# Expert gathers of 8 KB rows into one ring, in groups of two slots, in a decoder-step kernel on one core

## The reference, cut to what matters

```
q = (x @ w_query).reshape(t, 8, 2, 128);  s = einsum('thcd,ckd->thck', q, sub_keys)
sv, si = top_k(s, 16)                          # 16 best of 128 keys, twice a head
cand = sv[:, :, 0, :, None] + sv[:, :, 1, None, :];  top_s, pos = top_k(cand, 16)
experts = ...;  g = softmax(top_s)
u = expert_u[experts];  v = expert_v[experts]  # rows of 1024 float32, 4 KB each
a = gelu(einsum('td,thkd->thk', x, u))
out = einsum('thk,thkd->td', g * a, v)
```

## Time and profile before

| what | value |
|---|---|
| runs | 4222.06, 4222.38, 4271.96 us |
| span of the profiled execution | 4238.2 us |
| busy in the span | PE 81%, DVE 56%, POOL 56%, ACT 20% |
| DMA | 1320.95 MB, mean 312 GB/s |
| prompt front alone, ahead of tile 0 | 256.6 us |
| tile 7, 3564 to 4165 us | PE busy 502.5 of 601 us, DMA share 0.82 |
| one tile of the loop | 463 to 482 us (from one copy of `pick_cur` at L1316 to the next: 256.6, 737.5, 1200.6, 1675.3, 2149.4, 2618.9, 3093.0, 3564.0) |

### The profile page before, as it was taken

The page is one execution under the profiler, slowest core; times in us unless marked ns, Lnnn a source line. Parts: engine busy times, 40 slices in busy tenths (PEclk is TensorE's granted clock), DMA queues, the critical chain, the costliest instruction groups (busy, mean ns, idle before and its releaser), DMA issues.

```text
span 4238.2 us, 46989 instructions
## 1 busy us (share of the span) xinstructions
PE 3438.5 (81%) x13488; PEld 1997.5 (47%) x13488; DVE 2356.8 (56%) x5378; ACT 867.9 (20%) x2023; POOL 2390.2 (56%) x2071
## 2 busy tenths in 40 slices
PE   7749887798869886997879886998879886989874
PEld 5625453455435543654435543644445443733341
DVE  2464457455854476444854476455844466255666
ACT  1111211222121212122122212121122212122211
POOL 0036565666656575666656575665666566355642
PEclk9879998899989998998989998998889988699976
DMA  4369799989989798989989898989989898788884
GB/s 161 105 218 373 270 352 348 335 309 355 393 293 355 268 371 318 372 289 337 387 292 357 288 382 303 371 300 328 367 315 348 296 382 317 258 306 294 290 299 165
DMA packets 540672, 1320.95 MB, mean 312 GB/s; under 512 B 59252, under 2 KB 271774, under 8 KB 540376
## 3 DMA queue, kind: packets, MB, share of 16 engines
q0 software_dynamic: 297216, 1082.26, 69.2%
q1 hardware_dynamic: 239636, 229.70, 16.5%
q10 hardware_dynamic: 3524, 5.57, 0.4%
HBM read 1311.77 MB, written 5.62 MB: 311 GB/s over the span
## 4 chain that ended last, share of the span: by engine, by line
PE 42%; DVE 28%; issue 16%; another core or an unknown queue 5%; DMA 4%; ACT 4%; SPq 1%; DVEq 1%; POOL 0%; ACTq 0%; POOLq 0%
PE acc L690 18%; DVE u_ring L1280 12%; PE front L419 7%; PE front L526 3%; PE front L575 3%; DMA w_ring<-in_w_o 2%; PE front L547 2%; ACT diag L939 2%; PE front L527 2%; DVE si_u L1181 1%; DVE sv L1180 1%; PE front L650 1%; DMA w_ring<-in_w_in 1%; DVE work L1181 1%
## 5 line engine op out<-in xcount | busy, mean ns | idle before, releaser
L690 PE MATMUL acc<-v_ring,diag 128*128 128x512 f32 x3880 | 1889.3, 642 | 278.5 <-ACT diag L939 216.7
L1427 POOL DMA_INDIRECT v_ring<-in_expert_v,pick_cur x1024 | 1243.2, 1214 | 1054.9 <-PE acc L690 720.2
L1427 POOL DMA_INDIRECT u_ring<-in_expert_u,pick_cur x1024 | 1122.9, 1097 | 740.3 <-issue 306.5
L690 PEld LDWEIGHTS acc<-v_ring,diag 128*128 128x128 f32 x3880 | 781.0, 207 | 1251.2 <-issue 1137.8
L1280 DVE CUSTOM_DVE_ANT_0 u_ring<-u_ring,xn_cur 128x1024 f32<-128x1024 f32 x1024 | 1198.7, 1221 | 110.7 <-DMA u_ring<-in_expert_u,pick_cur 82.0
L419 PE MATMUL front<-work,w_ring 128*128 128x128 f32 (+1 forms) x4896 | 632.2, 285 | 74.7 <-issue 48.9
L419 PEld LDWEIGHTS front<-work,w_ring 128*128 128x128 f32 x4896 | 613.4, 204 | 103.6 <-issue 74.4
L930 ACT ACTIVATE gelu<-dots 128x4 f32<-128x4 f32 x256 | 52.6, 206 | 1508.1 <-DVE dots L1280 1401.6
L939 ACT ACTIVATE diag<-ident,wgt 128x128 f32<-128x128 f32 x970 | 310.4, 390 | 139.0 <-DVE wgt L1286 126.9
L575 PE MATMUL front<-w_ring,work 128*128 128x256 f32 (+1 forms) x576 | 158.2, 444 | 66.4 <-DVE work L1148 32.7
L1180 DVE MAX8 sv<-work 128x8 f32<-128x128 f32 (+1 forms) x288 | 83.2, 289 | 200.6 <-issue 113.9
(11 more groups left out here) (245 smaller groups left out, 2592.0 us busy)
## 6 DMA issues: line engine op xcount, KB each, us to landing
w_ring<-in_w_in SPq DMA_DIRECT2D x72, 1024.0 KB
w_ring<-in_w_query SPq DMA_DIRECT2D x72, 1024.0 KB
w_ring<-in_w_o SPq DMA_DIRECT2D x36, 1024.0 KB
u_ring<-in_expert_u,pick_cur POOLq DMA_INDIRECT x1024
v_ring<-in_expert_v,pick_cur POOLq DMA_INDIRECT x1024
work<-in_cache_ckv SPq DMA_DIRECT2D x64, 128.0 KB
w_ring<-in_w_in SPq DMA_DIRECT2D x9, 768.0 KB
x_t<-in_x_prompt SPq DMA_DIRECT2D x8, 512.0 KB
```

The costliest lines, as they stand in the source:

```text
L690: last = nc.tensor.matmul(acc[:, half, :], diag[:, slot, :], v_ring[:, slot, half * 512:half * 512 + 512], start=False, stop=(g == GROUPS ...
L1427: pool.indirect_dma_start(ring[:, slot, :], None, a[table][0], bass.IndirectOffsetOnAxis(ap=pick, axis=0)).then_inc(loaded[slot], 16)
```

## The change

Ahead of the launch, `expert_u` and `expert_v` are laid side by side in one table with rows of 8 KB. The kernel has one ring of 8 slots of 8 KB (`uv_ring`; `u_ring` and `v_ring` are its halves), one semaphore a slot and one gather a slot. That gather waits until the v product of the slot eight before is done. `G` goes from 4 to 2, so a tile has 64 groups of two slots; the order within a group stays as it was, and so does the number of slots in the ring, 8. `beside` now puts a prompt stage beside every second group (norm 0, turn 2, latent 4, ..., query 0 to 4 at 40 to 48, select 0 at 50, query 5 to 8 at 52 to 58, select 1 at 60) and, in tile 7, one stage beside each of the groups 0 to 61. The samples' mixer at the end gathers 8 rows of 8 KB a partition, all of them after the last v product of tile 7.

```diff
-G = 4
+G = 2
 GROUPS = SLOTS // G
-RING = 2 * G
+RING = 8
+ROUNDS = SLOTS // RING
...
-        u_ring = sb("u_ring", [P, RING, D])
-        v_ring = sb("v_ring", [P, RING, D])
+        uv_ring = sb("uv_ring", [P, RING, 2 * D])
...
+        u_ring, v_ring = uv_ring[:, :, 0:D], uv_ring[:, :, D:2 * D]
...
             def v_group(it, g):
                 for r in range(G):
-                    slot = (g % 2) * G + r
-                    if by_vector(it, g * G + r):
+                    s = g * G + r
+                    slot = s % RING
+                    if by_vector(it, s):
                         continue
-                    pe.wait_ge(on.diag_made, tensor_slots(it, g * G + r))
-                    pe.wait_ge(v_loaded[slot], (it * (GROUPS // 2) + g // 2 + 1) * 16)
+                    pe.wait_ge(on.diag_made, tensor_slots(it, s))
+                    pe.wait_ge(uv_loaded[slot], (it * ROUNDS + s // RING + 1) * 16)
...
-                act.wait_ge(on.v_free, RING + tensor_slots(it, (g - 1) * G - 1))
+                act.wait_ge(on.v_free, RING + tensor_slots(it, (g + 1) * G - 1 - RING))
...
             def dot_group(it, g, first=0, end=G):
                 for r in range(first, end):
-                    slot = (g % 2) * G + r
-                    dve.wait_ge(u_loaded[slot], (it * (GROUPS // 2) + g // 2 + 1) * 16)
+                    slot = (g * G + r) % RING
+                    dve.wait_ge(uv_loaded[slot], (it * ROUNDS + (g * G + r) // RING + 1) * 16)
...
-            def gather_group(it, g, table, ring, loaded):
-                if g * G == SLOTS // 2:
-
-                    pool.wait_ge(on.picks_moved, it + 1)
-                for s in range(g * G, (g + 1) * G):
-
-                    if table == "expert_u":
-                        pool.wait_ge(on.u_free, it * SLOTS + s + 1)
-                    elif by_vector(it, s - RING):
+            def gather(slot, pick):
+                pool.indirect_dma_start(uv_ring[:, slot, :], None, a["expert_uv"],
+                                        bass.IndirectOffsetOnAxis(ap=pick, axis=0)).then_inc(uv_loaded[slot], 16)
+
+            def tile(it):
+
+                pool.wait_ge(on.picked_moved, it + 1)
+                for s in range(SLOTS):
+                    if s == SLOTS // 2:
+
+                        pool.wait_ge(on.picks_moved, it + 1)
+                    if by_vector(it, s - RING):
                         pool.wait_ge(on.v_free_vector, vector_slots(it, s - RING))
                     else:
                         pool.wait_ge(on.v_free, RING + tensor_slots(it, s - RING))
                     waited(pool)
-                    gather(table, ring, s % RING, loaded, pick_cur[:, s:s + 1])
-
-            def tile(it):
-
-                pool.wait_ge(on.picked_moved, it + 1)
-                gather_group(it, 0, "expert_u", u_ring, u_loaded)
-                for g in range(GROUPS):
-                    if g + 1 < GROUPS:
-                        gather_group(it, g + 1, "expert_u", u_ring, u_loaded)
-                    gather_group(it, g, "expert_v", v_ring, v_loaded)
+                    gather(s % RING, pick_cur[:, s:s + 1])
...
+    arrays["expert_uv"] = np.concatenate([arrays.pop("expert_u")[0], arrays.pop("expert_v")[0]], axis=1)
```

More of the change, by code:

```diff
@@ L145, in build @@
         w_loaded = [ctx.enter_context(nc.semaphore(f"w_loaded{r}")) for r in range(WR)]
-        u_loaded = [ctx.enter_context(nc.semaphore(f"u_loaded{r}")) for r in range(RING)]
-        v_loaded = [ctx.enter_context(nc.semaphore(f"v_loaded{r}")) for r in range(RING)]
+        uv_loaded = [ctx.enter_context(nc.semaphore(f"uv_loaded{r}")) for r in range(RING)]
         pages_loaded = [[ctx.enter_context(nc.semaphore(f"pages_loaded{i}{q}")) for q in range(QUARTERS)] for i in range(2)]
@@ L812, in _ @@
             for t in range(SB):
-                pe.wait_ge(v_loaded[t], (TILES * (GROUPS // 2) + 1) * 16)
+                pe.wait_ge(uv_loaded[t], (TILES * ROUNDS + 1) * 16)
                 for half in range(2):
@@ L1298, in sum_group @@
                     dve.wait_ge(on.w_made, it * GROUPS + g + 1)
-                    dve.wait_ge(v_loaded[s % RING], (it * (GROUPS // 2) + g // 2 + 1) * 16)
+                    dve.wait_ge(uv_loaded[s % RING], (it * ROUNDS + s // RING + 1) * 16)
                     if vector_slots(it, s) > 1:
@@ L1407, in _ @@
             for t in range(SB):
-                dve.wait_ge(u_loaded[t], (TILES * (GROUPS // 2) + 1) * 16)
+                dve.wait_ge(uv_loaded[t], (TILES * ROUNDS + 1) * 16)
                 v.tensor_tensor_reduce(u_ring[:, t, :], u_ring[:, t, :], SPREAD[t], 1.0, 0.0, ALU.mult, ALU.add,
@@ L1424, in _ @@
             pool.memset(krT[:], 0.0).then_inc(on.zeroed, 1)
-            def gather(table, ring, slot, loaded, pick):
-                pool.indirect_dma_start(ring[:, slot, :], None, a[table][0],
-                                        bass.IndirectOffsetOnAxis(ap=pick, axis=0)).then_inc(loaded[slot], 16)
-            def gather_group(it, g, table, ring, loaded):
-                if g * G == SLOTS // 2:
-                    pool.wait_ge(on.picks_moved, it + 1)
-                for s in range(g * G, (g + 1) * G):
-                    if table == "expert_u":
-                        pool.wait_ge(on.u_free, it * SLOTS + s + 1)
-                    elif by_vector(it, s - RING):
+            def gather(slot, pick):
[7 more added lines that the diff above has]
+                    if by_vector(it, s - RING):
                         pool.wait_ge(on.v_free_vector, vector_slots(it, s - RING))
@@ L1459, in _ @@
             pool.wait_ge(on.u_free, TILES * SLOTS + RING)
-            for t in range(SB):
-                gather("expert_u", u_ring, t, u_loaded, s_pick[:, t:t + 1])
             pool.wait_ge(on.v_free, RING + tensor_slots(LAST, SLOTS - 1))
@@ L1464, in _ @@
             for t in range(SB):
-                gather("expert_v", v_ring, t, v_loaded, s_pick[:, t:t + 1])
+                gather(t, s_pick[:, t:t + 1])
 IN_NAMES = ["x_prompt", "x_sample", "cache_ckv", "cache_krope", "state_conv", "page_table", "g_mix_norm", "w_in", "g_q",
```

## The result

| | median us | runs | ratio to before |
|---|---|---|---|
| before | 4222.65 | 4 | |
| changed | 4394.37 | 4 (4382.60 to 4396.05) | 1.036 [1.031, 1.042] |
| changed, on another chip | 4402.99 (before there 4215.30) | 6 | 1.045 [1.041, 1.049] |

Slower by 172 us where 378 were forecast. The profiled execution's span went from 4238.2 to 4380.8: +142.6, of which the seven loop tiles take 135.0 (3307.4 to 3442.4, 472.5 to 491.8 us a tile) and the last tile with the tail 7.6 (forecast: -4). In that last stretch PE is busy 19.8 us longer (534.6 to 554.3) and idle 12.2 us less.

What follows compares the result with a forecast made beforehand. PE (396.4 of 474 us busy a tile) and its waits on DVE were taken to set the pace. Seven tiles of 42 + 13 make 385, with -10 and +6 +381: 4619, less 15.8 for the median, 4600 us; range 4370 to 4830.

Steps and rivals of the forecast that it cites:

- The cover step: Groups of two leave 3.5 us of products to hide DVE's stage parts; PE's idle time by DVE grows +42 a tile.
- Its list: PE's idle time stage by stage in one tile, such as 3.5 us for each of seven queries; sum 91 us.
- The level of 101 us: PE's idle time by DVE in one loop tile after the change, 91 + 10, up from 62.5.
- The tile's start: From tile to tile, four dots instead of eight ahead of the first product: 10 us idle instead of 20.
- Gathers 0, bounds -8 to 0: Per tile, one 8 KB gather instead of two gains nothing, because PE, not the transfer, sets the pace.
- The other 15 us I leave as they are: PE's idle time in a tile not put down to DVE, 6.8 of it a weight piece in mix_out: unchanged.
- Clock: After longer waits PE's products run at a lower clock: +13 us a tile, 5.5 more such waits at 2.4.
- The guess of half the queries: Half the queries, with 3.5 us idle each, were taken to cool PE's clock; bounds 2 and 9 more waits.
- Rival A: Starved weights: PE waits for weight pieces whose 1 KB rows queue beside 8 KB rows; 4850 us, chance 0.16.
- Rival C: No change to speak of: other stalls vanish, no query cools the clock, +21 a tile; 4344 us, chance 0.12.
- The last tile: Tile 7, with a stage beside every group, -10 (-25 to +15); the samples' gathers at the end +6.

Runs made afterwards that it cites:

- run 3: The kernel before with groups of two slots, its two tables, two rings and 4 KB rows kept: 4503.19 us, ratio 1.066.
- Run 1: The changed kernel with weights and diagonals of two neighbouring groups (four slots) made together ahead of the stage in the loop tiles: 4072.76 us, ratio 0.966.
- run 16: The kernel before with three fills of 800 elements behind each of DVE's 31 stage parts of a tile: 4506.29 us, ratio 1.070.
- run 10: The changed kernel with weights in fours and a POOL filler of 1.2 us ahead of each 8 KB gather: 4142.04 us.
- run 14: The changed kernel, still in groups of two, with a POOL filler of 1.2 us ahead of each gather: 4426.56 us, ratio 1.051.
- run 2: The changed kernel with u and v in two tables again and two 4 KB gathers per slot, one ring: 4478.28 us, ratio 1.062.
- run 9: The same kernel as run 1 (weights in fours, one 8 KB gather per slot), on another chip: 4077.30 us, ratio 0.985.
- run 11: The kernel of run 9 with two 4 KB gathers per slot instead of one of 8 KB: 4172.97 us.
- run 4: The changed kernel with weights made for four slots and two 4 KB gathers per slot, one ring: 4202.54 us, ratio 0.997.
- run 17: The changed kernel with weights in fours in the last tile too, not only the loop tiles: 4076.08 us, ratio 0.967.

## Why the direction was right and the size was not

The forecast is 35.7 us a tile too high: it put the gain of the gathers and the change in the other waits at nothing (17.0 and 10.0 of it) and sized the clock and the cover too large (4.5 and 4.3). Per loop tile, in us; run 3 has the grouping alone:

| term | forecast | grouping alone (run 3) | rows, ring | whole change |
|---|---|---|---|---|
| PE idle by DVE | +42 | +37.7 | -8.1 | +29.6 |
| PE's other waits | 0 | -10.0 | -1.7 | -11.7 |
| PE busy (clock) | +13 | +8.5 | -7.1 | +1.4 |
| sum | +55 | +36.3 | -17.0 | +19.3 |

- **The cover step held.** Its list met the trace: query 3.5 (3.3 to 4.3 found), mix_norm 10.8 (10.64), two dots and weights behind a search 3.1 (3.01). The level of 101 us was 105 in run 3 and 97 in the changed kernel. Run 1 gave it back by cover alone, run 16 raised it by longer stages alone. The tile's start was put at 10 idle and is 11.65.
- **"Gathers 0, bounds -8 to 0" failed.** Rows and ring together are worth -17 a tile in twos (traces of two chips), twice the lower bound. I reasoned that PE sets the pace, so a gather's price is hidden. But PE waits for DVE, and DVE for rows: an earlier row makes the next weights earlier at every stage with a wait behind it. POOL was ruled out as not the bound by its busy share; its 1.1 us per request are on that chain all the same (runs 10 and 14). The rows' own part was underestimated too: 8 ns for each packet removed (the figures given beside it make 7), where 8 KB now take 0.303 us against 0.316 before, 13 ns less, and against 0.322 in run 2 with the same grouping, 19 ns less. The Trainium skill (DMA: Bandwidth & Descriptors, Anatomy of one DMA) had the sign right where I had set it aside, but its 2.0 us a slot would be, as an estimate, 256 us a tile. One gather was worth 61 us in 1024 slots, 0.06 us a slot, and 96 in fours. Nor does a slot land sooner behind its request. The gathers of runs 9 and 11 (median us from issue to landing last):

```profile
uv_ring<-in_expert_uv,pick_cur POOLq DMA_INDIRECT x903, 9.6
```
```profile
uv_ring<-in_expert_u,pick_cur POOLq DMA_INDIRECT x901, 6.4
uv_ring<-in_expert_v,pick_cur POOLq DMA_INDIRECT x901, 7.0
```

  The one gather takes 9.6 us. The two take an estimated 8.4 from the first request to the second's landing (7.0 and the 1.4 by which the second is requested later: 1.12 of POOL's work and 0.3 idle). So, as the prediction said, the gain is not in one slot's duration; the error was to take what is left for nothing.

- **"The other 15 us I leave as they are" failed.** They fell by 10 with the grouping alone, at 4 KB rows. Not by pace (run 16). One account was that requests bunch: four products on end free four v slots and four dots four u slots, so POOL asks for some 4 MB in a row while weight pieces wait, and in twos for half of it. The traces speak against it. In run 3 POOL keeps the order of four u, then four v, and issues these eight on end (2134.17 to 2144.04 us in its timeline, then 6.30 idle); run 4 has its products in fours and yet few front waits. What did change in run 3 is POOL's wait for DVE ahead of its u requests, first before, then run 3 (loop, total us, times, longest):

```profile
POOL u_ring L1427 <- DVE dots L1280: 99.2, 16, 13.4
```
```profile
POOL u_ring L1429 <- DVE dots L1282: 1038.7, 144, 17.8
```

  Longer pauses behind each bunch would fit run 3, but no run tests them, and the cause stays open.
- **Clock.** +13 was +8.5 in run 3: products became slower by 16.1 us a tile (1721.4 to 1833.9), but the front's matmuls faster by 7.5 (those of L575 from 126.4 to 101.3), with the waits ahead of them gone or moved to the products. I counted only the new waits. In the changed kernel the two nearly cancel (+11.6 and -10.2). The guess of half the queries was fair: of the 49 waits of 3 to 4 us ahead of products in its loop, 25 left the next eight matmuls under 4 us (3.60 when warm); none of the 56 longer ones did.
- **Rival A had the opposite sign.** Weight pieces were waited for less, not more, and 8 KB rows did not starve them; in run 1 front waits are 1.5 a tile. Rival C came close for a tile (its 21 against 19.3) for partly the right reason: it let the other stalls vanish, but had no gain from the gathers, and its last tile at -25 was +7.6. It had 0.12.
- **The last tile**: -4 forecast, +7.6 found, within its bounds; fours there changed nothing (run 17), so its cause is open. PE's busy time rose there by 19.8 us, so it is not added idle time.

## What to carry over

An engine with idle time can still be on the path. Ask whether the bound engine's waits go back through it, and price each request it issues there, however small its busy share. When a term takes waits away or adds them, redo every wait of the same engine, not only those that the change names, because they move together: here the front's waits fell and the clock's loss moved from the front's matmuls to the products. A change with two parts should be forecast as two kernels: here one part was worth +287 us and the other about -110, and keeping the good one with weights in fours gave 0.966 (0.985 on another chip).

## Not expected of the hardware

The kernel before took 4216, 4131, 4142, 4215 and 4214 us beside the five groups of runs (runs 5 to 12 on one chip), 2% apart, while the fours with 8 KB rows (runs 1, 9 and 17) took 4073, 4077 and 4076. So ratios move with the chip (0.966 and 0.985 for one kernel), and small effects have to be compared on one chip, side by side. Why the one varies and the other does not is open. Thirty-two empty instructions on DVE cost nothing measurable; a fill of 800 elements there took 0.725 us, one of 600 on POOL 0.61.
